# The first MLP's second matrix by seven block products in three of four quarters, x kept in memory meanwhile, and the second modulation's parts spread anew

## The reference

```python
def sq_relu_mlp(h, w1, w2):
    return jnp.square(jax.nn.relu(h @ w1)) @ w2
...
    c_act = jax.nn.silu(c)
    for i in range(DEPTH):
        mod = c_act @ ada_w[i] + ada_b[i]
        sh1, sc1, g1, sh2, sc2, g2 = jnp.split(mod, 6, axis=-1)
        h = modulate(rmsnorm(x, norm_mix_g[i]), sh1, sc1)
...
        x = x + g1[:, None, :] * y
        h = modulate(rmsnorm(x, norm_mlp_g[i]), sh2, sc2)
        x = x + g2[:, None, :] * sq_relu_mlp(h, mlp_w1[i], mlp_w2[i])
```

## Time and profile before

| | us |
|---|---|
| median of 3 runs (lowest to highest) | 1779.81 (1778.88 to 1783.43) |
| the profiled execution | 1781.88 |
| its span in the trace | 1780.6 |
| TensorE busy in the span | 1731.3 (97%) |
| VectorE busy | 1161.8 (65%) |
| ScalarE busy | 715.4 (40%) |

### The profile page before, as it was taken

How to read it: one execution, slowest core, us unless ns; L and a number is a source line. 1 busy time by engine, 2 the same in 40 slices (tenths; PEclk the granted TensorE clock), 3 DMA queues, 4 the chain that set the end, 5 groups by cost and what they waited for, 6 DMA issues and landing times. The chain is left out here.

```text
span 1780.6 us, 22709 instructions
## 1 busy us (share of the span) xinstructions
PE 1731.3 (97%) x9313; PEld 1403.3 (79%) x9313; DVE 1161.8 (65%) x1391; ACT 715.4 (40%) x877; POOL 101.2 (6%) x114
## 2 busy tenths in 40 slices
PE   7899999999999999999999998999999999999997
PEld 4478888888888788888888786777888888888886
DVE  4465774478455655757547767775668668578578
ACT  4343113412333353535345533444544344344344
POOL 0100110010000010000000011110000000000000
PEclk9899999999999999999999999999999999999999
DMA  9942662266222337354312232002443435336324
GB/s 368 363 157 95 236 234 97 95 235 225 83 86 80 118 99 209 98 163 137 123 49 77 78 95 69 5 2 97 141 118 106 150 99 142 123 91 185 100 71 130
DMA packets 136343, 232.79 MB, mean 131 GB/s; under 512 B 14781, under 2 KB 50261, under 8 KB 136240
## 3 DMA queue, kind: packets, MB, share of 16 engines
q1 hardware_dynamic: 120368, 185.42, 31.2%
q0 software_dynamic: 15728, 45.33, 9.8%
q10 hardware_dynamic: 144, 0.59, 0.1%
HBM read 228.16 MB, written 4.73 MB: 131 GB/s over the span
## 5 line engine op out<-in xcount | busy, mean ns | idle before, releaser
L2163 DVE TENSOR_TENSOR w_lo<-raw,w_hi 128x2048 fp32r<-128x2048 f32 x105 | 240.6, 2292 | 240.8 <-ACT w_hi L1553 240.4
L1553 ACT ACTIVATE w_hi<-raw 128x2048 fp32r<-128x2048 f32 x109 | 208.5, 1913 | 373.3 <-PE bank L723 313.0
L723 PE MATMUL bank<-h_hi,w_hi 128*128 128x512 f32 x736 | 291.4, 396 | 6.9 <-DVE h_lo L2210 2.9
L723 PE MATMUL bank<-h_hi,w_lo 128*128 128x512 f32 x736 | 288.2, 392 | 0.0
L723 PE MATMUL bank<-h_lo,w_hi 128*128 128x512 f32 x736 | 288.1, 391 | 0.0
L723 PE MATMUL bank<-f_hi,w_hi 128*128 128x512 f32 x496 | 193.0, 389 | 0.0
L723 PE MATMUL bank<-f_lo,w_hi 128*128 128x512 f32 x496 | 193.0, 389 | 0.0
L723 PE MATMUL bank<-f_hi,w_lo 128*128 128x512 f32 x496 | 192.9, 389 | 0.0
L723 PEld LDWEIGHTS bank<-h_hi,w_hi 128*128 128x128 f32 x736 | 139.1, 189 | 41.6 <-issue 9.2
L723 PEld LDWEIGHTS bank<-h_hi,w_lo 128*128 128x128 f32 x736 | 139.0, 189 | 29.3
L723 PEld LDWEIGHTS bank<-h_lo,w_hi 128*128 128x128 f32 x736 | 139.2, 189 | 28.5 <-issue 0.5
(11 more groups left out here) (451 smaller groups left out, 3019.2 us busy)
## 6 DMA issues: line engine op xcount, KB each, us to landing
raw<-in_mlp_w SPq DMA_DIRECT2D x102, 512.0 KB, 4.7
ada_ring<-in_ada_w SPq DMA_DIRECT2D x12, 2048.0 KB, 15.1
ada_ring<-in_ada_w POOLq DMA_DIRECT2D x24, 1024.0 KB, 5.6
raw_more_mlp<-in_mlp_w SPq DMA_DIRECT2D x32, 512.0 KB, 4.7
raw<-in_w_ffn_up SPq DMA_DIRECT2D x32, 512.0 KB, 5.0
raw_more_ffn<-in_w_ffn_up SPq DMA_DIRECT2D x32, 512.0 KB, 4.9
raw<-in_w_in SPq DMA_DIRECT2D x20, 512.0 KB, 4.6
raw<-in_w_ffn_down SPq DMA_DIRECT2D x20, 512.0 KB, 4.7
```

Of the source, the lines that this page charges most:

```text
L723: mm = te.matmul(bank[:, n], a, b, start=first and k == 0 and j == 0, stop=last and k == 3 and j == 2, skip_group_check=s == SLABS["ffn"] + 1)
L1553: se.activation(m.ring(s)[0], m.raw_place(s), ACT.Copy).then_inc(sem("hi_made"), 1)
L2163: ve.tensor_tensor(lo, m.raw_place(s), hi.bitcast(F32), ALU.subtract).then_inc(sem("lo_made"), 1)
```

## The change

The first MLP is now done like the second: four quarters, three of them with the seven products, the fourth plain. It has 41 places in the order of slabs instead of 32 (32 loads from SP, and in each of three quarters a sum of VectorE's for two of them), so that all later slabs have numbers higher by 9. The functions of the second MLP take the layer as a parameter. What this needs:

- **Raw slots 2 and 3** in the first MLP lie in xT itself. x is written to memory (`x_saved`, 2 MB) by SP after the load of the last modulation block, and read back (`x_back`) once the fourth quarter has begun; slabs 4 and 5 wait for the save and for the norm's last reader.
- **u** goes from the relu straight to `quarter_u_mlp` and is squared there on ScalarE; `tmp` is for the sums of blocks.
- **Blocks 10 and 11 of the first modulation** both stand on VectorE ahead of the split of slab 3.
- **The units of the second modulation**: none in the first quarter, 2, 2, 1 beside the first three slabs of quarters two and three, and 1, 2, 2, 2, 2, 2, 2, 1 beside the eight slabs of the fourth.
- **POOL** starts the unit loads only after block 11, then issues the first quarter's adds, and mixes later loads and adds.
- The transposes use three banks instead of four, in both MLPs.

The core of the diff:

```diff
+ADA1_UNITS = {(1, 0): 2, (1, 1): 2, (1, 2): 1, (2, 0): 2, (2, 1): 2, (2, 2): 1, (3, 0): 1, (3, 1): 2, (3, 2): 2, (3, 3): 2,
+              (3, 4): 2, (3, 5): 2, (3, 6): 2, (3, 7): 1}
...
+        if s in (4, 5):
+            sy.wait_ge(sem("normed_lo"), 8)
+            sy.wait_ge(sem("x_saved"), 16)
...
             modulation(10)
             modulation(11)
+            sy.wait_ge(sem("x_mixed"), 8)
+            sy.dma_start(t["x_saved"], m.xT[:, :, :].rearrange("p k t -> p (k t)")).then_inc(sem("x_saved"), 16)
+        elif s == stage_slab("mlp0", 3, 1):
+            sy.wait_ge(sem("hi_made"), stage_slab("mlp0", 3, 0))
+            sy.wait_ge(sem("lo_made"), stage_slab("mlp0", 3, 0))
+            sy.dma_start(m.xT[:, :, :].rearrange("p k t -> p (k t)"), t["x_saved"]).then_inc(sem("x_back"), 16)
...
         product(stage, q, "a11", "b11", 4, updated(q - 1, "u3_21"))
+        if stage == "mlp0":
+            te.wait_ge(sem("mod_made"), 12 + q)
         product(stage, q, "s1", "t1", 6, updated(q - 1, "y"))
...
+                    slab_done(s + k)
+            if q < plain:
+                products(stage, q, g0 + 2 * q + 1)
...
+                modulation(q, 2 * g)
                 split_to(s + 2)
+                if layer == 0 and q == 0:
+                    if g == 0:
+                        ada_blocks(10)
+                        ada_blocks(11)
...
+                modulation(q, 2 * g + 1)
                 split_to(s + 3)
...
             for k in range(2):
                 split_to(s + k + 1)
+                modulation(plain, 4 + 2 * g + k)
...
+    ge.wait_ge(sem("ada_step"), sum(ADA_STEPS))
+    load(0)
+    load(1)
+    add("mlp0", 0, "s1", 1, 1)
+    add("mlp0", 0, "s3", 1, 0)
+    for q in range(1, QUARTERS["mlp0"]):
+        loads(5 * q - 3, 5 * q - 2)
+        add("mlp0", q, "s1", 1, 1)
+        loads(5 * q - 2, 5 * q + 2)
+        add("mlp0", q, "s3", 1, 0)
+    loads(5 * QUARTERS["mlp0"] - 3, ADA1_LOADS)
```

More of the change, by code:

```diff
@@ L391, in __init__ @@
         s, place = stage(self)
-        self.quartered = {"mlp1": Quartered(place, self.tmp, "mlp1")}
+        self.quartered["mlp1"] = Quartered(place, self.tmp, "mlp1")
         s.close()
[L394 to L397, removed]
         s, place = stage(self)
@@ L556, in mlp_quartered @@
             out += linear(w1, 2, (2 * q, 2 * q + 1))
-            out += products("mlp1", q) if q < QUARTERS["mlp1"] else linear(w2, 2, range(2), 2 * q)
+            out += products(f"mlp{layer}", q) if q < 3 else linear(w2, 2, range(2), 2 * q)
         return out
[L560 to L563, removed]
     def ffn():
@@ L934, in before_k, with after_n @@
                         normed(norm, 4 * k + kk)
+                    def after_n(n):
+                        if q == plain and g == 0:
+                            for o in turned.get((k, n), ()):
+                                rows_back(layer, o)
                     def after_k(kk):
@@ L963, in mlp0, with before_n, before_k, after_n @@
-        keep_busy(SLABS["sgu_in"], 7)
-        norm_mean(next_norm, sq)
+                    after_n(3)
+                    slab_done(s + k)
+            if q < plain:
+                products(stage, q, g0 + 2 * q + 1)
+        for g in range(2):
+            group, s = g0 + 8 + g, stage_slab(stage, plain, 4 + 2 * g)
+            for k in range(2):
+                def before_n(n):
+                    emptied(group - 1, n)
+                def before_k(kk):
+                    te.wait_ge(sem("u_hi_made"), 8 * layer + 4 * k + kk + 1)
+                    te.wait_ge(sem("u_lo_made"), 8 * layer + 4 * k + kk + 1)
+                def after_n(n):
+                    if n == 2 and layer == 0 and g + k == 2:
+                        ada1_sum(ADA1_LOADS)
+                slab(s + k, group, st.plain_hi[:, 4 * k:4 * k + 4], st.plain_lo[:, 4 * k:4 * k + 4], k == 0, k == 1,
+                     before_k if g == 0 else None, before_n, k_outer=g == 0 and k == 0, after_n=after_n)
+                slab_done(s + k)
@@ L977, in ada1_sum @@
         ada1["summed"] = until
-    def ada1_beside(w):
-        ada1_sum(sum(2 - i % 2 for i in range(w)))
-    mlp0(NORM_MLP0, NORM_MIX1, m.u_hi, m.u_lo, m.sq_b, ada1_beside)
+    norm_spread(NORM_MLP0)
+    ada_rows(7)
+    ada_sums(7)
+    mlp(0, NORM_MLP0)
+    keep_busy(SLABS["sgu_in"], 7)
+    norm_mean(NORM_MIX1, m.quartered["mlp0"].squares)
     keep_busy(SLABS["sgu_in"], 6)
@@ L2559, in vector_program, with ada1_add @@
     ada1 = {"added": 0}
-    def ada1_add(k):
-        for _ in range(2 - k % 2):
+    def ada1_add(units):
+        for _ in range(units):
             u = ada1["added"]
```

414 lines of the change are left out of this document (167 added, 247 removed).

## The result

The changed kernel takes 1795.12 us (median of 4 runs, 1793.04 to 1797.60) against 1781.62 for the kernel before (median of 4): ratio 1.0077, with a 95% interval of 1.0052 to 1.0101. Slower by 0.8%: 13.5 us where 5.4 were forecast.

A forecast was written before the change was run, and what follows sets the result against it. TensorE was taken to bound the kernel, busy 1731 of 1780.6 us. Terms −16.3 + 3.5 − 2.4 + 9.8 + 1.0 + 7.3 + 2.5 = +5.4 gave 1785.2 us against the median; range 1773 to 1796.

The forecast's parts named there:

- rival 5: First MLP: unit loads land in 8.0 us instead of 5.5 in each of six rounds, 1792 to 1797; chance 0.22.
- Matmuls, transposes, old gaps: TensorE, first MLP: 72 fewer matmuls −16.3, 32 added transposes +3.5, two old gaps gone −2.4; together −15.2 us without new stalls.
- The stalls of the first and fourth quarters: TensorE waiting for VectorE: +7.3 us before a11 and s1 in the first quarter, +9.8 in the fourth.
- The term of the fourth quarter: TensorE waits for VectorE before slabs 3, 5 and 6: stalls of 1.7, 1.3 and 6.8, together +9.8 us.
- that for loads: Unit loads that collide with slab loads: +1.0 us, with +13 as the far end.
- the 13.9 us: First quarter: VectorE's work from the adds' landing, s2 through slab 5's low part, before TensorE gets s1: 13.9 us.
- In quarters two and three the same adds wait for a unit only, with over 5 us to spare: s1's accumulating loads in quarters two and three come in time: no stall priced there.
- the clock's term: TensorE at half clock behind stalls: +2.5 us, 1.7 for the fourth quarter's 6.8 stall and 0.8 for the first quarter.
- x put aside: SP's 2 MB save of x ahead of slab 2's raw: cost 0; if late, +1 to +2 us at slab 2.
- the middle: First quarter: the adds land at 126.0, between near and far bounds; s1 stalls +7.3 us.
- the far bound: First quarter: the adds land behind 2 MB of unit loads, at 128.0; s1 stall at most +9.3 us.
- Rival 3: Fourth quarter: no stall, 1772.7 us; chance 0.12. Against it: VectorE's order is fixed, the update can't pass the units.

The follow-up runs named there:

- e8: Changed kernel with first-quarter adds ahead of the modulation, three units beside the second up slab with loads ahead of adds, one fourth-quarter unit moved earlier: 0.9957, 1775.47 us.
- e11: The changed kernel run again unaltered, as a reference: 1.0066 to the kernel before.
- e7: Changed kernel with the last seven units cut to one multiplication each on VectorE, loads and order kept: 1.0026 to the kernel before.
- e1: Changed kernel with the first quarter's two s1 adds issued on POOL before the modulation wait and two unit loads: 1.0024 to the kernel before.
- e2: Changed kernel with the fifth unit of quarters two and three moved behind the update p1 on VectorE: 1.0093 to the kernel before.
- e5: Changed kernel with the fifth unit of quarters two and three beside the second up slab, and unit loads ahead of s1's adds: 1.0032 to the kernel before.
- e4: Changed kernel with TensorE's three long gaps filled by 24, 9 and 22 matmuls whose results nobody uses: 1.0044 to the kernel before.
- e10: e8 with a new fourth-quarter order (update ahead of the unit, last sums behind the last slab) and x saved behind slab 3's load: 0.9968 to the kernel before.
- e3: Changed kernel with the fourth quarter's update of x ahead of the two units beside the second down slab: 1.0073 to the kernel before.
- e6: Changed kernel with one fourth-quarter unit moved from ahead of the update to beside the first up slab: 1.0035 to the kernel before.

## Why the prediction was right or wrong

**Right in sign and in its range, at the edge of it.** 1795.12 lies inside 1773 to 1796, but the sum said 1785.2. The stage grew by 15.6 us in the trace, where 3 to 6 stood under "what the profile will show". The measured time lies where rival 5 had put it, 1792 to 1797, and there by luck: of its six rounds of late unit loads the fourth quarter of this trace has one, of 1.36 us.

**What held.** Matmuls, transposes, old gaps: −15.2, borne out by e8. The stalls of the first and fourth quarters stood where they were forecast. The term of the fourth quarter and that for loads, 9.8 + 1.0, stand against 10.7 (gaps of 1.47, 1.03 and 6.46 and the 1.7 of low clock between them). From the quarter's start to the third down slab it was 84.1 us for 82.6, and 1.36 of the difference is the unit's load. In e11 it was 86.5, with 2.21 of load and 1.6 of low clock ahead, so that +1.0 for the loads fits this trace by luck, and e7 shows them as a bound of their own. Of VectorE's chain in the first quarter the 13.9 us are exact in three traces (e1).

**The first step that failed** is the sentence "In quarters two and three the same adds wait for a unit only, with over 5 us to spare". It was true of the adds, and I had looked at slabs and a11, not at s1. VectorE's order to s1 in these quarters has the same sums as in the first, and ahead of them the fifth unit (3.91 us) and a wait of 7.34 us for a unit load behind the adds: late by 2.47 and 1.65. That is +4.1, with 1.8 of clock +5.9, and it was priced at 0. e2 shows that without the unit there s1 isn't late; the load's landing earlier, as in e5, could have done it too, and no run has it alone.

**The second is the clock's term**, +2.5 by forecast, 9.2 in the trace. Of the 9.2, 1.5 between a11 and s1 and 1.7 at 415 stand ahead of a wait for VectorE and only make that wait shorter; e4 shows it for the 1.5. The other 5.9 lengthen the run: 1.8 behind s1, 1.8 behind the unforeseen wait at 231, 2.3 in the fourth quarter, of which I had 0.8 and 1.7. The Trainium skill, "TensorE: Matmul & The Clock Gate", "HAM oscillation — how this bites in real kernels", has the re-warming paid after each gap; this trace agrees for the first quarter's second part (1.8), which I had counted at less. In e11, where the second gap is 0.87, the clock behind it is full.

**The third is "x put aside", at 0.** Counted from the stage's first slab, slab 2's raw is in at 14.3 us before and in e10, where the save stands later. Behind the save it is in at 20.2 in e11 and at 24.0 in the first trace. ScalarE takes it at 22 at the earliest, so most traces hide the delay; in this one and in e1's it comes through, by 2 us. That s1 began 10.2 us late here (gaps of 0.55, 5.95 and 2.22 and the 1.5 between) for 7.3 forecast is mostly this. In e11 it was 8.1 late: there VectorE went on at 53.1, between the middle (51.9) and the far bound (53.9).

With 2.9 more for the first quarter, 4.1 for the unforeseen wait and 3.4 more for the clock, the forecast's +5.4 becomes +15.8, for 15.6 measured in the stage.

**Rival 3 and its control.** e3 shows why a stall on an engine that is full can't be ordered away: 6.46 us of gap became 8.14. e6 moved a unit into real idle time and won. The forecast had this right as "the update can't pass the units" but drew the line at the wrong place: what can't be passed is VectorE's sum.

Open: why slab 2's raw came 4 us later in two of the traces than in the others.

## What to carry to other kernels

When work is put beside a stage, look for each wait of the bounding engine in that stage, not only for the stage's total and its first wait: a 3.9 us unit at one place of VectorE's order cost up to 2.5, at its neighbour, with its load issued earlier, nothing. An idle stretch is room only if what stands behind it isn't wanted at once; ask who is released by it. A gap on TensorE can cost more than its length, by the low clock behind it: fill it, or add what the trace shows behind such gaps. But a low clock ahead of a wait for another engine costs nothing, and filling there wins nothing. And trace the same kernel twice before a difference of 3 us is explained.

## What the hardware showed unexpectedly

Accumulating loads hold the DMA engines far longer than their bytes say. In the window from 192 to 196 the engines are busy 1.06 and move 188 GB/s; with plain loads 1.05 is 410. A unit load issued right behind two adds (189.60) landed in 14.1 us and the next (196.66) in 10.2, one ahead of them in 6.6. So adds and loads don't share evenly: the landing of the adds, 11.9 us with loads ahead and 8.1 us with none just ahead (e1), and that of the loads behind them depend on who comes first.

A gap of 1.03 us at 415 was followed by a granted clock of 0.66 over 415 to 420, while gaps of 1.65 at 318 and 1.47 at 390 were followed by full clock. In e8 the same gap of 1.02 us, at 397, cost none. In e11 a gap of 1.48 cost 1.6 us and that of 1.02 none. So short gaps can lower the clock, and it is not the gap alone that decides.
